# A decoder layer on one Trainium2 core: the opening's loads and its modulation pieces in another order

## The reference, cut to what matters

```python
def decoder_layer(x, c, conv_prefix, pool_prefix, n_valid, w_ada, b_ada, ...):
    mod = jnp.einsum("bd,de->be", jax.nn.silu(c), w_ada) + b_ada
    sh1, sc1, g1, sh2, sc2, g2 = jnp.split(mod[:, None, :], 6, axis=-1)
    h = x * (1.0 + sc1) + sh1
    mix, new_conv, new_pool, v_rows = mixer_block(h, ...)   # one input projection, three mixers, w_out
    x = layer_norm(DEEPNORM_ALPHA * x + g1 * mix, ln1_g, ln1_b)
    h2 = x * (1.0 + sc2) + sh2
    f = jnp.einsum("btf,fd->btd", jnp.square(jax.nn.relu(h2 @ w_up)), w_down)
    x = layer_norm(DEEPNORM_ALPHA * x + g2 * f, ln2_g, ln2_b)
```

## Time and profile before

| what | value |
|---|---|
| median of 3 runs | 2103.55 us (2102.32 to 2107.53) |
| the profiled execution's own time | 2103.45 us |
| its span in the profile | 2101.7 us |
| PE busy | 2052.0 us, 98% of the span |
| DVE, ACT, POOL busy | 67%, 43%, 68% |
| DMA over the span | 169 GB/s |

### The profile page before, as it was taken

How to read it: one execution, slowest core, us unless ns; L and a number is a source line. 1 busy time by engine, 2 the same in 40 slices (tenths; PEclk the granted TensorE clock), 3 DMA queues, 4 the chain that set the end, 5 groups by cost and what they waited for, 6 DMA issues and landing times.

```text
span 2101.7 us, 27949 instructions
## 1 busy us (share of the span) xinstructions
PE 2052.0 (98%) x10479; PEld 1720.9 (82%) x10479; DVE 1416.1 (67%) x1847; ACT 905.7 (43%) x1292; POOL 1439.6 (68%) x1101
## 2 busy tenths in 40 slices
PE   7899999999999999999999999999999999999996
PEld 5677887888997888888878888878888899999994
DVE  2555687695776455577887676888667676665577
ACT  3224213232213655455565454665445555444441
POOL 3345797873343677788888788888787866666663
PEclk9999999999999999999999999999999999999998
DMA  8796887973432545545445555444654533454341
GB/s 275 232 297 221 238 273 222 261 229 95 153 111 85 177 157 158 183 141 172 128 144 187 202 163 167 150 130 150 207 187 137 188 98 121 137 186 143 120 132 45
DMA packets 319953, 357.52 MB, mean 170 GB/s; under 512 B 12356, under 2 KB 251969, under 8 KB 319818
## 3 DMA queue, kind: packets, MB, share of 16 engines
q1 hardware_dynamic: 319818, 355.72, 54.1%
HBM read 321.22 MB, written 34.44 MB: 169 GB/s over the span
## 4 chain that ended last, share of the span: by engine, by line
PE 84%; DVE 8%; DMA 2%; POOL 2%; ACT 1%; issue 1%; SPq 1%; DVEq 0%; ACTq 0%
PE ps L1179 26%; PE ps L1181 26%; PE ps L1180 26%; PE ps L1443 2%; PE ps L1192 1%; POOL w_hilo L894 1%; DMA xt<-in_w_down 1%; PE ps L1300 1%; DMA acc<-in_w_ada 1%; PE ps L1319 1%; DVE hid_a L1906 1%; DMA w_mix<-xt 0%; DVE pair_sums L1926 0%; DVE pair_sums L1927 0%; DVE pair_sums L1925 0%
## 5 line engine op out<-in xcount | busy, mean ns | idle before, releaser
L894 POOL TENSOR_TENSOR w_hilo<-w_raw,w_hilo 128x512 fp32r<-128x512 f32 x890 | 1277.8, 1464 | 602.5 <-ACT w_hilo L975 602.1
L975 ACT ACTIVATE w_hilo<-w_raw 128x1024 fp32r<-128x1024 f32 x445 | 470.5, 1058 | 538.0 <-PE ps L1181 426.3
L1179 PE MATMUL ps<-hA,w_hilo 128*128 128x512 f32 (+1 forms) x1760 | 622.2, 354 | 7.0 <-ACT htmp L1051 3.2
L1180 PE MATMUL ps<-hA,w_hilo 128*128 128x512 f32 (+1 forms) x1760 | 620.2, 352 | 0.0
L1181 PE MATMUL ps<-hA,w_hilo 128*128 128x512 f32 (+1 forms) x1760 | 620.2, 352 | 0.0
L1179 PEld LDWEIGHTS ps<-hA,w_hilo 128*128 128x128 f32 x1760 | 332.1, 189 | 52.2 <-issue 7.2
L1180 PEld LDWEIGHTS ps<-hA,w_hilo 128*128 128x128 f32 x1760 | 332.1, 189 | 41.5
L1181 PEld LDWEIGHTS ps<-hA,w_hilo 128*128 128x128 f32 x1760 | 332.0, 189 | 41.3
L1996 DVE TENSOR_TENSOR acc<-acc,ps 128x512 f32<-128x512 f32 x270 | 178.3, 685 | 77.0 <-PE ps L1181 74.0
L1179 PE MATMUL ps<-w_hilo,hid_a 128*128 128x512 f32 x450 | 181.5, 403 | 4.4 <-ACT more_sums L1149 4.4
L1181 PE MATMUL ps<-w_hilo,hid_a 128*128 128x512 f32 x450 | 175.7, 391 | 0.0
(11 more groups left out here) (236 smaller groups left out, 2822.7 us busy)
## 6 DMA issues: line engine op xcount, KB each, us to landing
w_raw<-in_w_up SPq DMA_DIRECT2D x128, 512.0 KB, 4.1
w_raw<-w_mix SPq DMA_DIRECT2D x124, 512.0 KB, 3.3
w_raw<-in_w_down SPq DMA_DIRECT2D x97, 512.0 KB, 3.7
w_raw<-in_w_in SPq DMA_DIRECT2D x64, 512.0 KB, 4.9
xt<-in_w_ada SPq DMA_DIRECT2D x20, 1024.0 KB, 8.2
w_raw<-in_w_out SPq DMA_DIRECT2D x32, 512.0 KB, 4.5
xt<-x_norm SPq DMA_DIRECT2D x19, 512.0 KB, 5.6
xt<-in_w_down SPq DMA_DIRECT2D x36, 256.0 KB, 5.0
```

The lines of the kernel that those rows point to most:

```text
L894: ins = pool.tensor_tensor(W[:, g % SLOTS, 1, cols], raw[:, g % RAW, cols], W[:, g % SLOTS, 0, cols], ALU.subtract)
L975: act.activation(W[:, g % SLOTS, 0, :], raw[:, g % RAW, :], ACT.Copy).then_inc(hi_done, 1)
L1179: pe.matmul(out, w_hi, x_hi, start=start, stop=False)
L1180: pe.matmul(out, w_hi, x_lo, start=False, stop=False)
```

## The change

It reorders SP's opening: piece 0's weights come ahead of the tables, slab 1 ahead of piece 2, slab 2 ahead of piece 4, and slabs from there on alternate with pieces. Pieces 8 to 13 go into places that pieces 3, 2, 4, 5, 6 and 7 have left (`ADA_PLACE_OF`), and are loaded in the opening; from piece 14 on the place is that of piece u - 2, and the load stands one feature slab later than before. On PE the pieces, turns and transposes of the v phase move in between a v slab's token tiles (`opening_between`), and those of the feature phase into `fm_product`, ahead of feature blocks 2 and 6. B moves behind F1, and the wait for `bias_kept` to F2. On ACT `v_normal` of super 0 moves behind the copies of pieces 8 and 9, and ACT makes the high half of every odd feature block itself. The small copies for `wsS` leave the opening and go to super 1; the pooling weights are loaded by two DMAs behind slab 8, and POOL splits them behind the low part of slab 8.

```diff
-def ada_pieces_after(f):
+def ada_pieces_with(f):
     return [ADA_FIRST + 2 * f, ADA_FIRST + 2 * f + 1] if f < 4 else [ADA_FIRST + 4 + f]
+ADA_PLACE_OF = {6: 0, 7: 1, 8: 3, 9: 2, 10: 4, 11: 5, 12: 6, 13: 7}
+ADA_AHEAD = 14
+def ada_place_of(u):
+    return ADA_PLACE_OF[u] if u < ADA_AHEAD else u - 2
...
             def ada_weights(u):
                 if u >= 6:
-                    sp.wait_ge(ada_mm, 4 * (u - 5 if u < ADA_FIRST else u - 1))
+                    sp.wait_ge(ada_mm, 4 * ada_place_of(u) + 4)
...
+            ada_weights(0)
             for i, src in enumerate(tables):
                 sp.dma_start(gs[TAB[i]:TAB[i + 1], 0:P], src).then_inc(s_tab, 16)
-            ada_weights(0)
...
             slab(0, free=False)
             for t in range(4):
                 x0_load(t)
-            for u in range(1, 4):
-                ada_weights(u)
+            ada_weights(1)
             slab(1, free=False)
+            ada_weights(2)
+            ada_weights(3)
+            slab(2, free=False)
             ada_weights(4)
             ada_weights(5)
-            corners()
-            slab(2, free=False)
+            slab(3)
             ada_weights(6)
             ada_weights(7)
-            slab(3)
             sp.dma_start(xt[0:ST, 4, :], x_sample.rearrange("b t d -> (b t) d")).then_inc(xs_in, 16)
+            slab(4)
+            ada_weights(8)
+            ada_weights(9)
...
             slab(6)
+            ada_weights(12)
             sp.wait_ge(x_split, 8)
             sp.dma_start(g1row[:, 0:W_GMLP], bcast(sgu_b[0], P)).then_inc(bias_in, 16)
             slab(7)
+            ada_weights(13)
             slab(8)
+            pool_corners()
...
             def x0_affine(k):
                 act.wait_ge(x0_tr, k + 1)
                 act.wait_ge(ada_T, 2 * (k // 2) + 2)
...
+                if k % 2:
+                    act.activation(hA[:, 0, k, 0:GT], src, ACT.Identity, bias=shift, scale=scale).then_inc(x0_high, 1)
                 if k >= 2:
                     act.wait_ge(x_split, k - 1)
...
-                    if n == 4:
+                    if n == 4 and s:
                         for t in range(4):
                             v_normal(s, t, s + nt - 3)
                     if s == 0 and SLAB_FM <= n < SLAB_O:
-                        for u in ada_pieces_after(n - SLAB_FM):
+                        for u in ada_pieces_with(n - SLAB_FM):
                             ada_sums(u)
...
+                        if n == 4:
+                            for t in range(4):
+                                v_normal(s, t, s + nt - 3)
...
+            def opening_between(n, t):
+                if n == 3:
+                    if t == 0:
+                        sample_x0()
+                elif t == 0:
+                    ada_product(2 * n + 3)
+                elif t == 1:
+                    ada_turn(2 * n + 2)
+                    ada_turn(2 * n + 3)
+                elif t == 2:
+                    x0_transposes(2 * n + 2)
+                    x0_transposes(2 * n + 3)
+                elif n < 2:
+                    ada_product(2 * n + 4)
...
-            for n in range(3):
-                ada_product(2 * n + 2)
-                ada_product(2 * n + 3)
-                ada_turn(2 * n + 2)
-                ada_turn(2 * n + 3)
-                x0_transposes(2 * n + 2)
-                x0_transposes(2 * n + 3)
-                v_slab(0, n)
...
+            ada_product(2)
+            for n in range(4):
+                v_slab(0, n, opening_between)
...
                     for k in range(KD):
+                        if ada and k % 4 == 2 and k // 4 < len(ada):
+                            ada_product(ada[k // 4])
+                            if ada[k // 4] > ADA_FIRST:
+                                ada_turn(ada[k // 4] - 1)
                         ins = mm3(ps[:, bank + c, 0:b - a], w[:, 0, k, :], w[:, 1, k, :],
...
+                        if f == 2 and first:
+                            pe.wait_ge(bias_kept, 1)
...
-                        pe.wait_ge(bias_kept, 1)
```

More of the change, by code:

```diff
@@ L256, in mixer_stages @@
     if first:
-        out, u = [], ADA_FIRST
+        out = []
         for x in a:
             out.append(x)
[L260 to L267, removed]
+            if x == ("F", 1):
+                out.append(("B", 0))
+        a = out + [("E", N_ADA - 1)]
+    return a
 def decoder_layer_kernel(nc, x_prompt, x_sample, c_prompt, c_sample, state_conv, state_pool,
@@ L592, in _, with pool_corners, sample_corners @@
                          state_pool[0].rearrange("b r c -> (b r) c")).then_inc(s_pre, 16)
-            def corners():
+            def pool_corners():
                 sp.wait_ge(s_prep, 1)
[L596 to L599, removed]
+                for half in range(2):
+                    q = 64 * half
+                    sp.dma_start(pool_raw[q:q + 64, :, q:q + 64],
+                                 pool_w[0].rearrange("(c two) i j -> two i c j", two=2)[half]).then_inc(s_corner, 16)
+            def sample_corners():
+                sp.wait_ge(s_prep, 2)
                 for b in range(NB):
[L601 to L604, removed]
+                    sp.dma_start(wsS[DT * b:DT * b + DT, :, DT * b:DT * b + DT], wsT[0:DT, :, 0:DT]
+                                 ).then_inc(corner_s, 16)
             def slab(g, free=True):
@@ L746, in _ @@
                     stage(1, 1)
-            for u in range(N_ADA - 3, N_ADA):
-                ada_rows_out(u)
+            ada_rows_out(N_ADA - 2)
             sp.wait_ge(ada_mm, 4 * N_ADA)
@@ L762, in _ @@
                     slab(MIX_SLABS * s + n)
+                    if n == 5 and s == 1:
+                        sample_corners()
                     if n == 9:
@@ L1233, in _, with v_slab @@
             ins.then_inc(s_prepe, 1)
-            def v_slab(s, n):
+            def v_slab(s, n, between=None):
                 nt = tiles_of(s)
@@ L1253, in v_slab @@
                         ins.then_inc(v_done, 1)
+                    if between and pos < nt - 1:
+                        between(n, t)
                 ins.then_inc(slab_used, 1)
+                if between:
+                    between(n, nt - 1)
             def x0_transposes(k):
@@ L1361, in mixer @@
                         pe.wait_ge(d_ready, 2 * s + c + 1)
+                        if first and c == 0:
+                            pe.wait_ge(s_prep, 3)
                         if c and nt == 5:
@@ L1853, in mixer @@
                         f = stage[1]
+                        if first and f == 2:
+                            dve.wait_ge(s_prep, 3)
                         work = {"u": u_fm, "pool": pool_fm}.get(FM_PARTS[f][0], conv_fm)
```

106 lines of the change are left out of this document (59 added, 47 removed).

## The result

The kernel with the change takes 2107.5 us (median of 20 runs, 2101.84 to 2109.99), the kernel before, run beside it on the same chip, 2103.31 us (2099.81 to 2108.08, 20 runs). The ratio is 1.0015, 95% interval 1.0009 to 1.0021. So the change costs 4.2 us by the medians and about 3.2 by the ratio (1.9 to 4.4), where 3.2 were to be saved. The result lies outside the range of 2095.0 to 2105.0, and on the other side of the kernel before. The profiled execution's own time is 2109.99 us, its span 2108.3; it is the slowest of the 20.

The account below looks back on a forecast made before the run. PE was taken to bound the kernel, busy 2052.0 us of 2101.7. The terms 0.7 + 0.5 - 3.0 - 1.2 - 0.6 + 6.2 + 1.8 - 1.2 gave 3.2 us saved from 2103.45: 2100.3 us, 80% range 2095.0 to 2105.0.

Parts of the forecast that it names:

- F2's new wait: At F2's start PE waits for DVE's part of F1 and the bias table: 1.2 us lost, between 0 and 2.
- v slab 3: Ahead of v slab 3 PE waits for the split of x: 1.2 us lost, bounds 0 and 1.9.
- ACT's order: Behind F0, piece 8 copied ahead of the normalisations removes PE's waits and the low clock there: 6.2 us saved.
- loads: At the start, x lands 2.0 us earlier and v slab 0 starts at 26.4, not 27.12: 0.7 us saved.
- clock: In v slab 0, the rise to the high clock level shortens the slow stretch: 0.5 us saved, between -0.7 and +1.0.
- switches: In v phase and F0 to F3, 15 more changes between small and big matmuls at 0.2 us each: 3.0 lost.
- Free switching, the first rival: Changes between small and big matmuls cost nothing, so 3.0 us come back: 2097.2 us, chance 0.17.
- Pieces 8 and 9: PE waits at piece 8 for DVE's split of the sample: 0.6 us lost, between 0 and 1.4.
- Piece behind piece: In three feature slabs, matmul blocks between pieces cover PE's wait of 0.61 for ACT's turned piece: 1.8 us saved.
- The small copies: In super 1, eight copies stand in SP's queue, covered by places ahead of PE: no cost, else 1 to 3 us.
- The clock rival: In the v phase, single tiles between small products keep the clock low: 2105.7 us, or 2114; chance 0.07.

Follow-up runs that it names:

- late_hi: On the kernel with the change, ACT makes slab 9's high part behind the copy of piece 12; 2101.25 us, ratio to the kernel before 0.9993.
- fill: On the kernel with the change, PE makes seven products nobody reads ahead of its wait at F2; 2102.3 us, ratio to the kernel before 0.9998.
- norm_only: The kernel before, with only ACT's normalisations of super 0's v moved behind the copies of pieces 8 and 9; 2098.7 us, ratio 0.998.
- bias_first: On the kernel with the change, DVE adds B to the bias table ahead of its part of F1; 2099.7 us, ratio to the kernel before 0.9983.
- f_back_bf: On `bias_first`, the pieces stand behind the feature slabs again, not inside them; 2099.91 us, ratio to the kernel before 0.998.
- x_early_bf: On `bias_first`, feature blocks 6 and 7 are transposed one token tile earlier in v slab 2; 2097.65 us, ratio to the kernel before 0.9971.
- spread_vf: On `bias_first` with both interleavings undone, the eight small copies are issued one behind each of eight slabs; 2096.45 us, ratio to the kernel before 0.9974.
- spread_xe: On `x_early_bf`, the eight small copies are issued one behind each of eight slabs; 2097.37 us, ratio to the kernel before 0.9975.

## Why the prediction was wrong, point by point

The forecast is 7.1 us off at super 1's transposes (3.2 earlier was said, 3.9 later was measured), and 7.4 by the medians.

- **F2's new wait (-1.2, bounds 0 and -2): the step that failed.** It measured 3.21, beyond its bound. The duration was taken from rows where POOL was idle: "3.3, and 0.7 for the bias table". I did say of v slab 3 that an operation of DVE can be slowed to 1.4, but didn't ask for F1 what POOL would do then. The change moved ACT's high part of slab 9 ahead of it, and that released POOL. With POOL away the wait was 1.44 (`late_hi`).
- **The clock in F2: not in the sum at all.** Rows 8 and 9 showed what an idle stretch of about 3.5 us does, and I counted the repair of the old one as a gain, but priced no new one, for the wait was to be short. It cost 4.4 (`fill`). That term is missing from the sum, and it is the larger of the two. Wait and clock are 2.0 and 4.4 beyond the forecast, together 6.4 of the 7.1 us between 3.2 saved and 3.9 lost.
- **ACT's order (+6.2): right, and shown alone.** `norm_only` gains 4.6 while it keeps B's two waits of 0.22 and 0.90 behind F0, together 5.7.
- **V phase (loads +0.7, clock +0.5, its part of the switches -1.8, v slab 3 -1.2, so -1.8): measured -2.3.** V slab 0 started at 27.72 and not 26.4, as x came at 17.43 and not 16.1. Piece 0 is issued 2.0 us earlier (1.56 for 3.56), but it only changed places with the tables, and x stands behind both as before: SP's queue shows the first load of x at 6.22 for 7.16, 0.94 earlier, and it landed 0.7 earlier. I had moved x by the 2.0 of piece 0; in the other kernels with this order x came between 16.14 and 17.36. The wait of v slab 3 was 1.26. V slabs 1 and 2 wait 0.26 and 0.25 for their splits as well, which I had taken as covered.
- **The switches.** Inside a slab of the kernel after, a group of small matmuls begins 0.32 behind the last big one (102.10 less 101.77 is 0.33), as before. Undoing both interleavings gains at most 1.1 us in the v phase, with v slab 3's wait of 1.26 in it, and loses about 0.9 in the feature phase. So what a switch costs rests on these rows; the medians can't resolve it. Free switching, the first rival, has the rows against it and no run that decides it.
- **Pieces 8 and 9 (-0.6): measured 0.92**, and 0 in `bias_first`, see below.
- **Piece behind piece (+1.8):** the three waits of 0.61 are gone, and `f_back_bf` brings them back; net of switches some 1 us.
- **The small copies, costed at nothing:** they held SP 6.0 us, the cover was not enough, and 0.6 to 0.7 us of PE's wait at super 2's transposes came of it, about 1.0 in the whole stretch.
- **The rivals.** The clock rival was on the right side with the wrong place: I looked for the low level in v slab 0, where it rose by 33.5, and it fell at F2. No load of the opening was late in the kernel after; the longest wait for one behind x is 0.98, for piece 1.

## What to carry to other kernels

A duration belongs to its neighbourhood: before a DVE row is used as a price, see whether POOL was idle beside it, and whether the change will release POOL there. A wait on PE near 3 us is not to be priced by its length alone, for what the clock took afterwards was larger here (4.4 for 3.2); the next section shows that it doesn't take it every time, so it belongs into the range as well as into the sum. When a large change should save little, look for its one part that the profile proves: the move of one loop on ACT brought nearly as much (0.998) as the best kernel of the study (0.997).

## What the runs showed of the hardware that was not expected

- **DVE beside POOL is slower by a factor of two and more, and it is a matter of timing.** The cast and the subtraction that piece 8 waits for, in the kernel after, while POOL works without a gap from 60.31 (8.07 us):

```profile
65.85 1.40 DVE L1680 CAST hA<-acc 128x512 fp32r<-128x512 f32 x1
67.28 1.66 DVE L1681 TENSOR_TENSOR hA<-acc,hA 128x512 fp32r<-128x512 f32 x1
```

and in `bias_first`, where POOL pauses for 0.91 us just there:

```profile
64.70 0.43 DVE L1682 CAST hA<-acc 128x512 fp32r<-128x512 f32 x1
65.17 0.69 DVE L1683 TENSOR_TENSOR hA<-acc,hA 128x512 fp32r<-128x512 f32 x1
...
65.30 2.94 POOL L923 TENSOR_TENSOR w_hilo<-w_raw,w_hilo 128x512 fp32r<-128x512 f32 x2 [0.91 <-ACT w_hilo L1006]
```

The pair takes 3.1 us or 1.1. Nothing was changed at this place between the two kernels; 0.9 us of PE's time hung on it. The subtraction of 0.69 had begun in the pause, 0.13 ahead of POOL, and then it was POOL's work that took longer, 2.94. In the kernel after DVE's operation that reads PSUM keeps its 0.42 at 62.62 and at 64.42, while POOL works too.
- **The low level came with one idle stretch of 3.21 us and held F2 until 101.3**, though PE was busy from 91.74 on; after 1.44 us of idleness it didn't come, each seen in one execution. A gap filled with products that nobody reads didn't bring it either.
- **The length of a wait didn't settle it.** All twelve traces hold one wait of PE of 3.24 to 3.27 us that ends between 1692 and 1706 us. Within 2 us of its end the granted clock falls to 0.50 in eight of them, and stays at 1.00 in `fill`, `norm_only`, `x_early_bf` and `spread_vf`. The wait of 1.96 to 1.98 us at super 2's transposes was followed by the low level in `bias_first`, `fill` and `f_back_bf`, and not in the kernel after, `late_hi` and `x_early_bf`.
- **Eight copies within SBUF held the queue for 6.0 us**, 0.75 each, where the load of a slab takes 0.37 to issue (52.08 in the kernel before). Issued one by one in `spread_xe` each still takes 0.74 to 0.86.
